# A two-stack transformer block on one core: the opening pool stage rearranged, and a quarter-wise subtraction on GpSimd

## The reference, cut to what matters

```python
def rmsnorm(x, g):
    y = x * lax.rsqrt(jnp.mean(x * x, axis=-1, keepdims=True) + EPS)
    return y * g
def pool_mixer(h, w, scale):            # h = rmsnorm(x, norm_mixer[0])
    csum = cumulative sum of h over the tokens
    for g, win in enumerate((2, 4, 8, 16)):      # 4 groups of 256 columns
        d[g] = (windowed mean of h over the last `win` tokens) - h
    return einsum('btgc,gce->btge', d, w) * scale
x = x + pool_mixer(...)
x = x + (silu(n @ w_gate) * (n @ w_up)) @ w_down     # n = rmsnorm(x, norm_ffn[0])
... attention, a second feed-forward, then a second block of two layers
```

## Time and profile before

| | us |
|---|---|
| median of 3 runs | 1136.82 |
| lowest, highest | 1136.5, 1138.36 |
| the profiled execution, first to last instruction | 1136.3 |

### The profile page before, as it was taken

One profiled execution on the slowest core, in us unless ns is written; L12 is line 12 of the kernel. 1 busy time (PEld: TensorE's weight loads), 2 busy tenths in 40 slices (PEclk: granted clock), 3 DMA queues, 4 the chain that ended last, 5 costly groups with the idle time before them and its releaser, 6 DMA issues. The chain is left out here.

```text
span 1136.3 us, 17002 instructions
## 1 busy us (share of the span) xinstructions
PE 1122.5 (99%) x6556; PEld 977.6 (86%) x6556; DVE 784.7 (69%) x1019; ACT 533.2 (47%) x702; POOL 107.5 (9%) x203
## 2 busy tenths in 40 slices
PE   9999999999999999999999999999999999999997
PEld 7888888898888888879998888888899988888886
DVE  6766666767667666677676676666766866766665
ACT  5533333556653334344585543343446755433332
POOL 1000000000000000002760000000037500000000
PEclk9999999999999999999999999999999999999999
DMA  8765556664356555668953565556697443665550
GB/s 254 262 206 197 178 196 207 223 200 147 114 167 222 186 191 179 214 150 258 233 159 112 166 223 185 185 184 201 174 254 179 132 149 127 214 209 191 184 185 37
DMA packets 176056, 211.23 MB, mean 186 GB/s; under 512 B 22371, under 2 KB 158947, under 8 KB 176002
## 3 DMA queue, kind: packets, MB, share of 16 engines
q1 hardware_dynamic: 166226, 202.89, 56.0%
q0 software_dynamic: 9776, 7.62, 3.7%
HBM read 201.98 MB, written 1.16 MB: 179 GB/s over the span
## 5 line engine op out<-in xcount | busy, mean ns | idle before, releaser
L683 ACT ACTIVATE whi<-raw 128x2048 fp32r<-128x2048 f32 x176 | 336.4, 1914 | 382.2 <-PE bank L1608 245.5
L999 DVE TENSOR_TENSOR wlo<-raw,whi 128x2048 fp32r<-128x2048 f32 x171 | 391.3, 2290 | 156.6 <-ACT whi L683 156.5
L1604 PE MATMUL bank<-h_both,whi 128*128 128x512 f32 x1280 | 304.6, 390 | 0.0
L1604 PEld LDWEIGHTS bank<-h_both,whi 128*128 128x128 f32 x1280 | 237.7, 188 | 47.7
L1578 PE MATMUL bank<-whi,o_hi 128*128 128x512 f32 x448 | 176.2, 393 | 0.0
L1579 PE MATMUL bank<-wlo,o_hi 128*128 128x512 f32 x448 | 174.9, 390 | 0.0
L1580 PE MATMUL bank<-whi,o_lo 128*128 128x512 f32 x448 | 174.4, 389 | 0.0
L1608 PEld LDWEIGHTS bank<-h_both,wlo 128*128 128x128 f32 x1280 | 164.1, 191 | 6.2
L1608 PE MATMUL bank<-h_both,wlo 128*128 128x256 f32 x1280 | 166.0, 283 | 0.0
L1580 PEld LDWEIGHTS bank<-whi,o_lo 128*128 128x128 f32 x448 | 84.1, 188 | 17.9
L1578 PEld LDWEIGHTS bank<-whi,o_hi 128*128 128x128 f32 x448 | 84.3, 188 | 17.6 <-issue 1.3
(11 more groups left out here) (210 smaller groups left out, 1345.2 us busy)
## 6 DMA issues: line engine op xcount, KB each, us to landing
raw<-in_w_gate_up SPq DMA_DIRECT2D x44, 1024.0 KB, 5.1
raw<-in_w_down SPq DMA_DIRECT2D x44, 1024.0 KB, 4.9
raw<-in_w_gate SPq DMA_DIRECT2D x22, 1024.0 KB, 5.4
raw<-in_w_up SPq DMA_DIRECT2D x22, 1024.0 KB, 5.3
raw<-in_w_in SPq DMA_DIRECT2D x20, 1024.0 KB, 7.7
raw<-in_w_o SPq DMA_DIRECT2D x12, 1024.0 KB, 5.4
raw<-in_w_kv SPq DMA_DIRECT2D x8, 1024.0 KB, 5.3
raw<-in_w_q SPq DMA_DIRECT2D x4, 1024.0 KB, 5.0
```

Of the source, the lines that this page charges most:

```text
L683: act.activation(whi[:, s, :], raw[:, s, :], ACT.Copy).then_inc(hi_ready, 1)
L999: dve.tensor_tensor(wlo[:, s, :], raw[:, s, :], whi[:, s, :].bitcast(F32), ALU.subtract).then_inc(lo_ready, 1)
L1604: pe.matmul(bank[bk + jj][:, :], hi[:, kc, jj * P:(jj + 1) * P], h_both[:, kc, :, :].rearrange("p a t -> p (a t)"), start=(kc == 0), stop= ...
```

## The change

Unlike before, the stage now runs as follows.

- SP asks for the band between the two tiles of x, and for the gain rows after x.
- Squares: ACT takes the first half of each tile (counting it twice), DVE the second half of each, so DVE has one more square, ahead of the first `mean_square`.
- The second tile's scaled band is written as one run of 128 columns for each group, by two DVE instructions (64 and 448 columns in all); PE takes it in one run.
- Pool weights: ACT and DVE take half 0, groups 0 and 1, half 1, groups 2 and 3. PE's products go (tile, group) = (0,0), (1,0), (0,1), (1,1), (0,2), (0,3), (1,2), (1,3).
- GpSimd writes the low part of unit 1 in four quarters of 128x512: one before the power of tile 0 of the first feed-forward norm, three between the powers of tile 0 and tile 1. DVE takes those of unit 2 in two halves instead, and waits for GpSimd's count before the second.
- `pool_add(1, 0)` goes ahead of `normalise(1, 0, ...)`, `pool_add(1, 1)` ahead of `h_lo_out(1, 0, 0)`. In the first feed-forward `first_glu` goes ahead of `split(u0 + 3)`.
- GpSimd asks for the one-hot table behind its first two powers. Fillers are 10, 5, 6 and 5; the 6 are new, ahead of the bias product.

```diff
-            for t in range(TT):
-                sp.dma_start(x[:, t, :], xv[t]).then_inc(x_in[t], 16)
+            sp.dma_start(x[:, 0, :], xv[0]).then_inc(x_in[0], 16)
+            sp.dma_start(band, c["c_band"].rearrange("p g n -> p (g n)")).then_inc(band_in, 16)
+            sp.dma_start(x[:, 1, :], xv[1]).then_inc(x_in[1], 16)
             sp.dma_start(gain_rows, GAIN_SRC[0].rearrange("(k p) -> k p", p=P)).then_inc(gains_in[0], 16)
-            sp.dma_start(band, c["c_band"].rearrange("p g n -> p (g n)")).then_inc(band_in, 16)
...
-            for v in range(4):
+            rsqrt(0)
+            pool.dma_start(onehots, c["c_onehots"]).then_inc(onehot_in, 16)
+            def first_gate_lo(q):
+                if q == 0:
+                    pool.wait_ge(hi_ready, FFN_U[0] + 1)
+                s, cols = slot_of(FFN_U[0]), slice(q * UNIT // 4, (q + 1) * UNIT // 4)
+                i = pool.tensor_tensor(wlo[:, s, cols], raw[:, s, cols], whi[:, s, cols].bitcast(F32), ALU.subtract)
+                if q == 3:
+                    pool.wait_ge(lo_ready, FFN_U[0])
+                    i.then_inc(lo_ready, 1)
+            first_gate_lo(0)
+            rsqrt_tile(1, 0)
+            for q in range(1, 4):
+                first_gate_lo(q)
+            rsqrt_tile(1, 1)
+            for v in range(2, 4):
                 rsqrt(v)
...
-            for t, h in ((0, 0), (0, 1), (1, 0)):
-                square(0, t, h, 2 if t else 1)
+            for t in range(TT):
+                square(0, t, 0, 2)
...
-            for part in range(2):
-                pool_whi(part)
             act.wait_ge(gcol_ready, 1)
             for k in range(4):
+                if k % 2 == 0:
+                    pool_whi(k // 2)
                 act.wait_ge(pool_d, k + 1)
...
-                        dve.wait_ge(acc_ready, no + 1)
+                        dve.wait_ge(acc_ready, (1, 3, 2)[no])
...
                     mean_square(1, 0)
+                    pool_add(1, 0)
                     normalise(1, 0, 0)
                     normalise(1, 0, 1)
-                    pool_add(1, 0)
                     pool_scale(1, 1)
+                    pool_add(1, 1)
                     h_lo_out(1, 0, 0)
-                    pool_add(1, 1)
                     h_lo_out(1, 0, 1)
-                    split_half(u0, 0)
                     mean_square(1, 1)
                     normalise(1, 1, 0)
                     normalise(1, 1, 1)
-                    split_half(u0, 1)
+                    split_half(u0 + 1, 0)
                     h_lo_out(1, 1, 0)
                     h_lo_out(1, 1, 1)
-                    split(u0 + 1)
+                    dve.wait_ge(lo_ready, u0 + 1)
+                    split_half(u0 + 1, 1)
...
+                if f == 0:
+                    first_glu()
                 split(u0 + 3)
-                first_glu()
+                if f:
+                    first_glu()
...
+                src = band.rearrange("p (g n) -> p g n", g=4)
+                dst = band_s[1].rearrange("p (g n) -> p g n", g=4)
+                for to, at, width in ((0, P + 16, 16), (16, 16, P - 16)):
+                    dve.tensor_scalar(dst[:, :, to:to + width], src[:, :, at:at + width], rstd[:, 1:2], None, ALU.mult).then_inc(xn_ready, 1)
...
+            second_half_square(0)
+            dve.wait_ge(last_square, 1)
             mean_square(0, 0)
+            second_half_square(1)
             scaled_band(0)
-            dve.wait_ge(last_square, 1)
+            dve.wait_ge(last_square, 2)
             mean_square(0, 1)
             scaled_band(1)
...
-            for part in range(2):
-                pool_wlo(part)
             dve.wait_ge(gcol_ready, 1)
             for k in range(4):
+                if k % 2 == 0:
+                    pool_wlo(k // 2)
                 dve.wait_ge(hT_hi, k + 1)
...
+                width, stride, at = (P, P, P) if s else (P + 16, BAND_W, 0)
...
+            for t, g in ((0, 0), (1, 0), (0, 1), (1, 1), (0, 2), (0, 3), (1, 2), (1, 3)):
+                if t == 0:
+                    if g % 2 == 0:
+                        pe.wait_ge((pool_lo, lo_ready)[g // 2], 1)
+                    pe.wait_ge(hT_lo, g + 1)
...
+            multiply_zeros(IDLE_MATMULS[2], 3)
             pe.wait_ge(ones_set, 2)
```

More of the change, by code:

```diff
@@ L45 @@
 BIG = 3.0e38
-IDLE_MATMULS = (10, 10, 5)
+IDLE_MATMULS = (10, 5, 6, 5)
 HD = 64
@@ L239, in bass_two_stacks @@
         band = band_flat[:, 0:4 * BAND_W]
-        band_s = [band_flat[:, (1 + i) * 4 * BAND_W:(2 + i) * 4 * BAND_W] for i in range(TT)]
+        band_s = [band_flat[:, 4 * BAND_W:8 * BAND_W], band_flat[:, 8 * BAND_W:8 * BAND_W + 4 * P]]
         gain_rows = xn[0:KC, 0, 0:P]
@@ L593, in _ @@
             pool.dma_start(tables[T5_ROW:T5_ROW + NBUCKET, 16:24], a["t5_table_2"]).then_inc(table_in, 16)
-            pool.dma_start(onehots, c["c_onehots"]).then_inc(onehot_in, 16)
             def rsqrt(version):
@@ L1320, in scaled_band, with second_half_square @@
                 dve.wait_ge(rstd_ready, t + 1)
-                dve.tensor_scalar(band_s[t], band, rstd[:, t:t + 1], None, ALU.mult).then_inc(xn_ready, 2)
+                if t == 0:
+                    dve.tensor_scalar(band_s[0], band, rstd[:, 0:1], None, ALU.mult).then_inc(xn_ready, 2)
+                    return
+                src = band.rearrange("p (g n) -> p g n", g=4)
+                dst = band_s[1].rearrange("p (g n) -> p g n", g=4)
+                for to, at, width in ((0, P + 16, 16), (16, 16, P - 16)):
+                    dve.tensor_scalar(dst[:, :, to:to + width], src[:, :, at:at + width], rstd[:, 1:2], None, ALU.mult).then_inc(xn_ready, 1)
+            def second_half_square(t):
+                dve.wait_ge(x_in[t], 16)
+                dve.tensor_tensor_reduce(xn[:, 1, t * HALF:(t + 1) * HALF], x[:, t, HALF:], x[:, t, HALF:], 1.0 / D, 0.0,
+                                         ALU.mult, ALU.add, ssq[:, t, 1:2]).then_inc(last_square, 1)
+            second_half_square(0)
+            dve.wait_ge(last_square, 1)
             mean_square(0, 0)
-            dve.wait_ge(x_in[1], 16)
-            dve.tensor_tensor_reduce(xn[:, 1, HALF:], x[:, 1, HALF:], x[:, 1, HALF:], 1.0 / D, 0.0, ALU.mult, ALU.add,
-                                     ssq[:, 1, 1:2]).then_inc(last_square, 1)
+            second_half_square(1)
             scaled_band(0)
-            dve.wait_ge(last_square, 1)
+            dve.wait_ge(last_square, 2)
             mean_square(0, 1)
@@ L1754, in _ @@
             for s in range(TT):
-                parts = [(P + 16, P, 16), (16, P + 16, P - 16)] if s else [(0, 0, P + 16)]
+                width, stride, at = (P, P, P) if s else (P + 16, BAND_W, 0)
                 pe.wait_ge(xn_ready, 2 * s + 2)
@@ L1758, in _ @@
                     for k in range(2):
[L1759 to L1763, removed]
+                        mm = pe.matmul(bank[g][:, k * T + at:k * T + at + width], x[:, s, g * 256 + k * P:g * 256 + (k + 1) * P],
+                                       band_s[s][:, g * stride:g * stride + width],
+                                       start=(s == 0 and k == 0), stop=(s == 1 and k == 1), skip_group_check=True)
                     if s:
@@ L1766, in _ @@
             hi, lo = w8(POOL_U)
[L1767 to L1777, removed]
+            for t, g in ((0, 0), (1, 0), (0, 1), (1, 1), (0, 2), (0, 3), (1, 2), (1, 3)):
+                if t == 0:
+                    if g % 2 == 0:
+                        pe.wait_ge((pool_lo, lo_ready)[g // 2], 1)
+                    pe.wait_ge(hT_lo, g + 1)
+                for k in range(2):
+                    mm = three(bank[ACC[2 * t + g // 2]][:, (g % 2) * 256:(g % 2) * 256 + 256],
+                               h_hi[:, 2 * g + k, tile(t)], h_lo[:, 2 * g + k, tile(t)],
+                               hi[:, 2 * g + k, :], lo[:, 2 * g + k, :], k == 0, k == 1)
+                if g % 2 and (t, g) != (1, 3):
+                    mm.then_inc(acc_ready, 1)
             used(mm)
+            multiply_zeros(IDLE_MATMULS[2], 3)
             pe.wait_ge(ones_set, 2)
@@ L1784, in _ @@
             pe.matmul(bank[6][0:24, :], tables[:, :], onehots, start=True, stop=True).then_inc(vec_done, 1)
-            multiply_zeros(IDLE_MATMULS[2], 3)
+            multiply_zeros(IDLE_MATMULS[3], 3)
             def ffn(f):
```

## The result

The changed kernel takes **1141.35 us** (median of 7 runs, 1139.96 to 1143.28) against 1136.82 before (7 runs in the same comparison, 1136.49 to 1138.36): ratio 1.0036, 95% interval 1.0027 to 1.0046. It is 4.5 us slower; 1136.5 was forecast and 1138.6 was the upper end of the range. The profiled execution of it took 1141.89, of which 1140.1 lie in the span: what lies around a span is 1.8 us in every run here. The profiled execution of the kernel before, with its span of 1136.3, thus took about 1138.1 (an estimate from that 1.8), 1.3 over the median of its runs, and the rows that the prediction starts from are of that execution.

A forecast was written before the change was run, and what follows sets the result against it. PE, busy 99%, was taken to set the time, which moves with tile 1's product and the wait at 43.83. The terms +0.2 and -0.5 sum to -0.3 on 1136.82: 1136.5 us, range 1134.5 to 1138.6.

The forecast's parts named there:

- The landing of tile 1 and of the gain rows: Opening loads: tile 1 of x and gain rows land behind the band at 6.7 to 7.3, taken as 7.05.
- Rival C: Opening: tile 1 or gain rows land at 7.6 or later, everything 0.5 us later, 1137.0; chance 0.10.
- B2: Before tile 0's product: PE waits some 2 us, clock falls to 0.5 for 3.41 us, costing 1.7: 1139.2; chance 0.07.
- The PE time gained is handed on to two engines that now bound it: Band to pool weights: PE gains 1.9 us, but ACT and DVE let `h_lo` end only 0.5 earlier.
- Band, weights in turn, order of products: Opening: 16 fewer band instructions save PE 1.9 us; `h_lo` ends at 16.45; the product order wins and loses nothing.
- rival D: Band: 16 instructions bound by columns, so the gain is 1.6, not 1.9; `h_lo` hides it, no price; no chance given.
- mostly fillers: Kernel before, 20 to 24 us: PE's busy time is mostly fillers, so DVE's chain counts ahead of 24.41.
- Blocking: First norm: GpSimd quarters and DVE instructions with two SBUF inputs wait for each other; tile 1's product +0.2 us.
- rival B: GpSimd takes each first turn: both `normalise` wait 1.2, tile 1's product +1.1, 1137.5; chance 0.20.
- the kindest order of turns: Tile 0's norm: DVE goes first and alternates with GpSimd, so only the second `normalise` waits 1.2 us.
- Behind tile 1: After tile 1's product: early `first_glu` removes PE's 0.34 wait at 43.83 and the drained pipeline: -0.5 us.
- lucky clock: Near 517.34 us: the clock's fall can come or stay away after a shift, 1.7 us either way.

The follow-up runs named there:

- b_loads: Kernel before with the band asked for between the tiles of x and the gain rows behind: 1139.64 us, ratio 1.0024.
- a_loads: Changed kernel with the order of loads undone (both tiles of x, gain rows, then band): 1138.28 us, ratio 1.0004.
- a_warm: Changed kernel with 20 instead of 10 fillers on PE ahead of the gain rows: 1139.07 us, ratio 1.0014.
- a_all3: Changed kernel with the old load order, unit 1's low part on DVE, and an early one-element square on ACT: 1135.13 us, ratio 0.9979.
- q_quarters: Changed kernel with the old load order and the early square on ACT, GpSimd's four quarters kept: 1137.24 us, ratio 1.0002.
- b_pool: Kernel before with only unit 1's low part in GpSimd quarters and unit 2's in DVE halves: 1139.37 us, ratio 1.0017.
- a_dve_loads: Changed kernel with the old load order and unit 1's low part on DVE, no early table load: 1135.63 us, ratio 0.9988.
- a_dve: Changed kernel with unit 1's low part back on DVE in two halves, late loads kept: 1137.05 us, ratio 0.9996.

## Why the prediction was wrong

**The landing of tile 1 and of the gain rows: the step that failed.** I took 512 KB behind the band at the pace of the second transfer, 1.3 us, and got 7.05. It was 8.2, and 8.5 for the gain rows (PE takes them at 8.54). The pace was that of the second place in line; the third place was in the trace of before and I didn't read it: the band, third then, was issued at 2.08 and took 5.2 us, so it landed at 7.3, 1.4 behind tile 1 for 320 KB, where 0.8 would have been the second place's pace. From about 5.5 us on the small loads, and from about 6 on the pool weights, share the way: tile 1 moved 75 packets of 4 KB in the microsecond from 5.0, and 39 in the 1.5 us from 6.0. Rival C named this ("land at 7.6 or later"), with a price of 0.5 us and a chance of 0.10. Its place was right and its price at least five times too small (2.5 us in b_loads, 3.1 between a_loads and the change).

**The price of PE's wait: not in the sum at all.** My own times leave PE idle for some 1.2 us ahead of the gain rows (from 5.8 to 7.05), and the sum has nothing for it. The row for it stood in my own B2: a clock at 0.5 behind waits. I applied it at 22 us and not at 6 us, where PE's clock had hardly risen. What it cost stands in the terms that I had at 3.8 for 32 band instructions, which took 5.60, and at 1.2 for five fillers, which took 2.50. a_warm measures it as 2.3 us of the whole kernel. "The PE time gained is handed on to two engines that now bound it" turned round: PE bounded ACT again (4.62 us of waits for L1790, ACT's h_hi from 15.31).

**The table load** was missed; I read `square` with a count of 2 as a mere number. With a count of 1 in front (before) the table is loaded at 0.75, ahead of the wait for x; with 2, behind it, at 4.78. My reading is that an instruction that adds 2 carries no wait of its own, so that the wait stands in front of the load; no run changes the count alone. It was covered by the late tile here; with the loads mended its price is not settled.

**Band, weights in turn, order of products: right** once the opening is mended. `h_lo` ends at 16.43 in a_all3, and 16.45 was forecast; that it is so near is in part luck, as the same program gave 15.75 to 16.89. The band's 32 instructions take 4.01 (3.8), which is 1.67 less than the 48, nearer rival D's 1.6 than my 1.9, and hidden as D said. Of PE's time between 20 and 24 us in the kernel before, fillers are only 1.4; my "mostly fillers" was wrong, and nothing hung on it, since it is DVE's chain that ends last there.

**Blocking: mechanism right, size too small.** The power took 0.94 (0.9 to 1.0 was said), the quarters 1.28 when undisturbed (1.1 to 1.4), the pair of `normalise` 3.38 where I had 2.5 (21.9 to 24.4). Quarter 0 met `pool_add(0, 0)` (1.73) and not `pool_add(0, 1)`, since `h_lo` was late; with the loads mended it is the latter (1.07 and 1.53). DVE didn't get the first turn; rival B had that, with 1.2 for each wait instead of the measured 0.98. From the end of `h_lo` to tile 1's product it was 13.31 before. My times add 0.7 to that (+0.2 at the product, with `h_lo` 0.5 early), rival B's 1.6, and the profiles with quarters show 2.1 in the changed kernel and up to 2.8 in q_quarters, where the clock fell as well. B2's fall came without B2's condition: I had put it at waits of some 2 us, and it came after 0.76 and 1.02, and elsewhere stayed away after the same waits. I summed the forecast from the kindest order of turns, and had no case in which the late loads and the turns come together.

**Behind tile 1: right.** From tile 1's product to the transposes of the activation it is 13.08 us (36.06 to 49.14), and it was 13.57 (30.26 to 43.83): -0.49, forecast -0.5. It is 13.06 to 13.08 in the other kernels too, except b_loads (13.58). But b_pool has it as well (32.92 to 45.98) without `first_glu` moved, so that moving it is the cause is not shown: the quarters alone also remove the wait.

**The sum.** Of the 5.8 us at tile 1's product 3.7 are there when `h_lo` ends (forecast -0.5), and 2.1 come behind it (forecast +0.7): the opening is 4.2 of the miss, the turns 1.4. +5.8 less the 0.5 behind makes 5.3; the profiled spans differ by 3.8, the medians by 4.5. Some 1.5 us come back at 514 us, for a reason of the single execution: before, PE waited 1.36 there and then ran at the lower clock; in the changed kernel the clock was lower from 516.23, while PE did tile 0's part, and the wait for tile 1 was hidden behind the slower work. That also explains most of 3.8 against 4.5, since the profiled execution of before was 1.3 above its median, and that of the changed kernel 0.5. PE's timeline of the changed kernel, and then the windows view of the stretch behind it (columns as above):

```profile
516.02 0.37 PE L1676 MATMUL bank<-whi,h_both 128*128 128x256 f32 x1 [2.06 <-ACT h_both L717]
```

```profile
516.23:519.64 3.41, 3.41 (x18) 3.41 (x18) 2.89 (x7) 1.47 (x5) 0.97 (x1) 0.50 0.80 248
```

What I called a lucky clock is thus a matter of where it falls. I didn't test this place.

**Shares.** Undoing the loads alone gives 3.1 us back, undoing the quarters alone 4.3, both together 5.7 (a_dve_loads), and all of it 6.2. From a_dve_loads upwards, the quarters add 2.6 (a_loads), the late loads 1.4 (a_dve), and both 5.7, which is 1.7 more than the sum of the two. Whether they really cost more together is not settled, as the runs of a_dve spread over 3.9 us. In the kernel before each added edit costs 2.5 and 2.2. Undoing both leaves a kernel 1.2 per mille faster than before, 2.1 with the early table load, which is the part of the change that does what it says: together the two causes cost more than the loss of 4.5, since the rest of the change pays some 1.5 to 2 us.

## What to carry to other kernels

Read a transfer's price from the place in line that it will have, and look up what else is on the way by then. An engine's wait at the start of a kernel isn't free if its clock has yet to rise: cover it with work that does nothing, or count the work behind it at the lower clock. A slower stretch of one engine costs only what the engine beside it doesn't hide: compare with a profile in which that stretch ran fast. One profile is one execution, so read a stretch behind a common point and not from the start of the kernel. Work given to GpSimd costs DVE whole instructions wherever DVE reads two SBUF operands: give it in small pieces, or beside DVE work that reads PSUM.

## What the runs showed of the hardware

- DVE instructions with two SBUF operands and GpSimd ones that read SBUF held each other up, and the wait went with the length of one GpSimd instruction: 0.98 us lost a turn against GpSimd instructions of 1.28 (128x512), 0.43 against 0.72 (128x256). DVE's instructions on PSUM and one SBUF operand kept their 0.68 between them (29.78 in the changed kernel).
- Ten matmuls of zeros more, while PE would have waited 2.44 us, saved 2.3 us: at the lower clock a 128x512 filler took 0.43 to 0.5 and a band instruction 0.17; at the higher one 0.24 and 0.12.
- The same waits of PE (0.7 and 1.02 us) were followed by a granted clock of 0.50 for 3.41 us in three profiles and not in a fourth. 16 products of 128x512 took 5.50 us in it instead of 3.88, and tile 1's product came 0.9 later.
- The clock column of the windows view reads 1.00 from the start of every one of these kernels, also where fillers take 0.43 us or more; ahead of its first change only the durations tell the level.
- A one-element square on ACT at 2.04 us moved the load of the table of functions from 4.58 to 0.75.
